# Four expert picks summed one query chunk earlier, and three groups of the state-space norm scaled by GpSimd

## The chip, the cores and the metric

The kernel runs on one core of a Trainium2 chip. The time is the device time of one execution in microseconds, as a median of several runs. The core's engines are TensorE (matrix products), VectorE, ScalarE and GpSimd (elementwise work; GpSimd also issues the gathers), and SyncE, which issues the other transfers. Each works through its own queue in order, and they wait for each other on semaphores. The profile calls them PE, DVE, ACT, POOL and SP.

## What is computed

Two decoder layers, all in float32, on 256 tokens of width 1024. The first one is a hybrid of gated linear attention and a state-space block, followed by a mixture of experts with product keys. The change touches the norm of the state-space block and the expert layer:

```python
y = y.reshape(Bsz, L, SSD_D_INNER) * jax.nn.silu(z)              # 2048 columns
y = rmsnorm(y.reshape(Bsz, L, SSD_GROUPS, SSD_D_INNER // SSD_GROUPS),
            ssd_norm_w.reshape(SSD_GROUPS, -1)).reshape(Bsz, L, SSD_D_INNER)   # 4 groups of 512
y_b = y.astype(hn.dtype) @ w_up_ssd
...
q = (hb @ w_q).reshape(n, PEER_HEADS, 2, PEER_HALF)              # 16 chunks of 128 query columns
s = jnp.einsum('nhid,hikd->nhik', q, sub_keys)
...                                                              # top 16 experts for each of 8 heads
u = jnp.take(u_tab, idx, axis=0)
act = jax.nn.gelu(jnp.einsum('nhkd,nd->nhk', u, hb))
out = jnp.einsum('nhk,nhkd->nd', w * act, jnp.take(v_tab, idx, axis=0))
```

The second part of the network (retention and stick-breaking attention) is not touched.

## The kernel before

All weights come as one stream of chunks of 128x1024 numbers. A chunk is loaded, split into a high half (ScalarE, line 1612) and a low half (VectorE, line 2072), and multiplied in three products (lines 1118 to 1120). Kind "T" chunks hold 128 columns (a chunk is 8 times 3 products of 256 columns), kind "N" chunks hold 512 columns of 256 rows. One generator, `order_of_work`, writes out the order of all steps once, and every engine's program walks the same list and issues its own part of each step. So a step's place in the list is its place in the queue of every engine that takes part in it. Side work is cut into strands, and a strand goes on at fixed places between the products of a chunk (`side_step`).

**The norm.** The gated features Y lie as two tiles of 128 tokens by 2048 columns. When a group's squares are summed (step `z`), VectorE computes the reciprocal root (step `y_root`, lines 1980 to 1992; groups 0 and 1 in one go, then 2, then 3) and multiplies the identity by it, once for each token tile: a diagonal (lines 1996 and 1997). TensorE then turns the features and scales them in one (step `yT`, sixteen of them, four in each group): two products of 128x128 float32 by the diagonal into a bank of PSUM, 4 to 7 in turn (lines 1383 and 1384). ScalarE and VectorE take high and low halves out of the bank (lines 1773 and 2287), and only then can the bank be used by the yT four places on. DY holds the diagonals of two groups, so the root of group 2 waits for the yT of group 0. The steps stand in this order: y_root 0 in chunk 83, y_root 2 and yT 0 and 1 in chunk 85, yT 2 and 3 in 86, yT 4 to 7 in 87, y_root 3 behind chunk 88, yT 8 and 9 behind 89, and so on. Chunks 73 to 88 are z, from 89 on comes the product with `w_up_ssd`.

**The expert layer.** A pick is one (token tile, head, rank): 256 picks, each for 128 tokens. GpSimd gathers 128 rows of 8 KB for it (line 2624), 1.05 MB, half of a row for the dot product and half for the sum. For each pick VectorE takes the dot (step `dot`, line 2371), ScalarE the gelu of four picks at a time (line 1823), VectorE multiplies by the softmax weights (step `weigh`, line 2376), ScalarE makes a diagonal of the weight (line 1831), and TensorE adds diagonal times rows to the output, two products of 512 columns (step `sum`, line 1434), each of which is two instructions. The gathers go into up to 17 slots. A slot is free for a new pick when the old pick's sum is done; slots that overlap the ring of split chunks are free when a certain query chunk has been multiplied. Before the change no sum stands in the list before the scores of the last two query chunks, step ("scores", 14, 2). The picks go into slots like this: picks 0 to 8 into slots 1, 2, 3, 7, 8, 6, 4, 5 and 0; 9 to 15 into slots 14, 10, 11, 12, 13, 15 and 16; pick 12 waits for chunk 14 of the query, 13, 14 and 15 for chunk 15; pick 16 goes into slot 9 (behind the scores of chunk 15), 17 to 20 into the slots of picks 0 to 3.

**The order around the last query chunks.** Chunk 14 (with the scores of 12 and 13 in its middle), dot 8, gelu of picks 4 to 7, gather 12; chunk 15, dot 9, weigh of 4 to 7, gathers 13 to 15; the scores of 14 and 15, dot 10, sums 0 to 7, gathers 16 to 24. The weights of picks 0 to 3 are made at dot 7, behind chunk 13. Scores are 8 products of 128x128 (line 1415); ScalarE copies each query chunk out of PSUM first (line 1801) and the scores afterwards (line 1810).

Of the kernel before, what the change touches and what calls it, by code (L numbers as in the profile page):

```python
# [11 lines left out]
ALU = mybir.AluOpType  # L12
# [165 lines left out]
def order_of_work():  # L178

    done = set()  # L180
# [416 lines left out]
    def peer_side():  # L597
# [28 lines left out]
        for m in range(256):  # L626
# [10 lines left out]
            if ("scores", 14, 2) not in done:  # L637
                for ms in waiting:
                    if ("weigh", *ms) not in done:
                        yield say("weigh", *ms)  # L640
            while waiting and ("scores", 14, 2) in done:
                yield from weighed()
# [280 lines left out]
def build(nc, stream, par, rows, con1, con2, xin, xt, meta, subk, peer_uv, out):  # L923
    ctx = ExitStack()
    with ctx:
# [19 lines left out]
        SM = sb("SM", [128, 512])  # L945
# [10 lines left out]
        def place(name, at, n):  # L956
            assert at + n <= ARENA, name
            return AR[:, at:at + n]
# [48 lines left out]
        ZS = place("ZS", 20944, 1024).rearrange("p (b c) -> p b c", b=2)  # L1007
        DY = place("DY", 0, 512).rearrange("p (b i c) -> p b i c", b=2, i=2)
        H = place("H", 25600, 2048).rearrange("p (i d) -> p i d", i=2)
# [102 lines left out]
        def tensor_program(pe, hi, lo, prod, side, act, dve, pool):  # L1112
# [38 lines left out]
            for step, *at in order_of_work():  # L1151
# [226 lines left out]
                elif step == "yT":  # L1378
                    f, = at
                    b, g, c = 4 + f % 4, f // 4, slice(128 * f, 128 * f + 128)  # L1380
                    on.wait_ge(*dve.of(("y_root", max(g, 1))))
                    bank(b)
                    pe.matmul(ps[b][:, 0:128], Y[:, 0, c], DY[:, g % 2, 0, :], start=True, stop=True)
                    pe.matmul(ps[b][:, 128:256], Y[:, 1, c], DY[:, g % 2, 1, :], start=True, stop=True).then_inc(*side.up(("yT", f)))
                    free[b] = dve.of(("yT", f))
# [585 lines left out]
        def vector_program(v, hi, lo, prod, side, act, dve, pool):  # L1971
# [58 lines left out]
            for step, *at in order_of_work():  # L2030
# [243 lines left out]
                elif step == "y_root":  # L2274
# [3 lines left out]
                    root(("y", g), SM[:, 16 + 2 * g:18 + 2 * groups[-1]], 512)  # L2278
                    if g >= 2:
                        on.wait_ge(*side.of(("yT", 4 * (g - 2) + 3)))  # L2280
                    for n in groups:
                        diagonals(("y_root", n), DY[:, n % 2, :, :], SM[:, 16 + 2 * n:18 + 2 * n])
                elif step == "yT":
# [317 lines left out]

        def pool_program(g, hi, lo, prod, side, act, dve, pool):
            on = Passed(g)
            uses = {}
            for step, *at in order_of_work():
                if step == "gather":
                    m, j, before = at
# [15 lines left out]
                    uses[j] = uses.get(j, 0) + 1  # L2623
                    g.indirect_dma_start(slots[j], None, peer_uv, bass.IndirectOffsetOnAxis(ap=IDX[:, i, c:c + 1], axis=0)).then_inc(s_uv[j], 16)  # L2624

# [230 lines left out]
```

## Time and profile before

| | |
|---|---|
| median of three runs | 1486.52 us (1486.42 to 1487.09) |
| profiled execution | 1488.33 us |
| its span, first to last instruction | 1486.5 us |
| TensorE busy | 1358.8 us, 91% |
| VectorE busy | 1064.0 us, 72% |
| ScalarE busy | 678.8 us, 46% |
| GpSimd busy | 298.0 us, 20%, all in issuing gathers |
| mean granted TensorE clock | 0.966 of full speed |

The profile is one execution. Its page gives the busy time of each engine, the span cut in 40 slices of 37 us, the chain of work that ended last, and groups of instructions by line. The trace behind it gives single instructions with start and duration, the idle time in front of each and the instruction that ended it. Times in it are us from the start of the span. The norm's steps lie between 306 and 342 us, the query chunks between 403 and 455, the picks between 417 and 1077.

### The profile page before, as it was taken

What the parts mean: (1) busy time and instruction counts of PE and PEld (TensorE: products, weight loads), DVE (VectorE), ACT (ScalarE), POOL (GpSimd) and SP (SyncE); (2) the same over time, 40 slices, a digit from 0 to 9 for tenths busy, and PEclk for the clock granted to TensorE, in tenths of its full rate; (3) what the DMA queues carried; (4) which work ended last, traced back from release to release, by engine and by line L of the source; (5) the groups of instructions that cost most, each with busy time, mean ns of one, the idle gap of its engine ahead of it and who ended that gap; (6) DMA issues with size and microseconds to landing.
All of it is one profiled execution on the core that took longest, in us unless ns stands there. A gap on an engine that the chain in (4) does not pass through costs nothing.

```text
span 1486.5 us, 18111 instructions
## 1 busy us (share of the span) xinstructions
PE 1358.8 (91%) x6713; PEld 980.8 (66%) x6713; DVE 1064.0 (72%) x2115; ACT 678.8 (46%) x1246; POOL 298.0 (20%) x260
## 2 busy tenths in 40 slices
PE   9999999999999887787878687788999999999998
PEld 9999989789895333333333233333499888998876
DVE  6977688766698777776777677665787665766664
ACT  7765976674553222222122222222364575645663
POOL 0000000000035554444435444443200000000000
PEclk9999999999999999998989989999999999999999
DMA  8444555445979999999999999999765555454542
GB/s 303 154 174 142 185 177 167 152 157 184 344 287 393 421 421 421 420 423 421 421 421 421 421 422 421 422 420 422 310 231 174 166 184 185 162 177 143 167 144 86
DMA packets 78487, 418.78 MB, mean 282 GB/s; under 512 B 8816, under 2 KB 9008, under 8 KB 45376
## 3 DMA queue, kind: packets, MB, share of 16 engines
q0 software_dynamic: 36864, 268.45, 43.6%
q1 hardware_dynamic: 41536, 149.17, 30.5%
q8 instruction: 54, 0.88, 0.2%
q14 instruction: 33, 0.27, 0.1%
HBM read 416.51 MB, written 1.08 MB: 281 GB/s over the span
## 4 chain that ended last, share of the span: by engine, by line
PE 58%; DMA 27%; DVE 9%; ACT 3%; issue 2%; POOL 1%; DVEq 0%; SPq 0%; POOLq 0%; ACTq 0%
DMA AR<-in_peer_uv,C 15%; PE ps L1118 14%; PE ps L1120 14%; PE ps L1119 14%; DMA SLAB<-in_peer_uv,C 12%; PE ps L1434 8%; DVE AR L2371 1%; DVE wlo L2072 1%; DVE SLAB L2371 1%; POOL SLAB L2624 1%; ACT whi L1612 1%; PE ps L1367 1%; POOL AR L2624 0%; ACT AR L1831 0%; DVE AR L2213 0%
## 5 line engine op out<-in xcount | busy, mean ns | idle before, releaser
L2072 DVE TENSOR_TENSOR wlo<-raw,whi 128x1024 fp32r<-128x1024 f32 x246 | 298.9, 1222 | 148.7 <-ACT whi L1612 148.0
L1434 PE MATMUL ps<-SLAB,AR 128*128 128x512 f32 x520 | 258.9, 650 | 59.5 <-ACT AR L1831 59.5
L1612 ACT ACTIVATE whi<-raw 128x1024 fp32r<-128x1024 f32 x246 | 258.9, 1057 | 118.8 <-PE ps L1120 103.7
L1434 PE MATMUL ps<-AR 128*128 128x512 f32 x504 | 248.3, 643 | 55.8 <-ACT AR L1831 55.6
L1118 PE MATMUL ps<-XH,whi 128*128 128x256 f32 (+1 forms) x896 | 261.6, 292 | 0.6 <-DVE XL L2312 0.6
L2624 POOL DMA_INDIRECT AR<-in_peer_uv,C x126 | 140.8, 1118 | 588.5 <-DVE C L2027 416.7
L1120 PE MATMUL ps<-XH,wlo 128*128 128x256 f32 (+1 forms) x896 | 254.2, 284 | 0.0
L1119 PE MATMUL ps<-XL,whi 128*128 128x256 f32 (+1 forms) x896 | 254.1, 284 | 0.0
L1434 PEld LDWEIGHTS ps<-SLAB,AR 128*128 128x128 f32 x520 | 105.3, 207 | 207.8 <-issue 125.3
L1434 PEld LDWEIGHTS ps<-AR 128*128 128x128 f32 x504 | 101.2, 205 | 197.2 <-issue 118.2
L2371 DVE CUSTOM_DVE_ANT_0 SLAB<-SLAB,AR 128x1024 f32<-128x1024 f32 x130 | 158.3, 1223 | 72.7 <-DMA SLAB<-in_peer_uv,C 72.7
L2371 DVE CUSTOM_DVE_ANT_0 AR<-AR 128x1024 f32<-128x1024 f32 x126 | 153.4, 1224 | 57.7 <-DMA AR<-in_peer_uv,C 57.7
L2624 POOL DMA_INDIRECT SLAB<-in_peer_uv,C x130 | 157.0, 1207 | 169.5 <-PE ps L1434 139.8
L1118 PEld LDWEIGHTS ps<-XH,whi 128*128 128x128 f32 x896 | 170.7, 191 | 2.9 <-issue 1.2
L1119 PEld LDWEIGHTS ps<-XL,whi 128*128 128x128 f32 x896 | 170.7, 191 | 1.5 <-issue 1.2
L1120 PEld LDWEIGHTS ps<-XH,wlo 128*128 128x128 f32 x896 | 170.6, 190 | 0.0
L1118 PE MATMUL ps<-whi,XH 128*128 128x512 f32 x416 | 170.4, 410 | 0.0
L1823 ACT ACTIVATE C<-C,SM 128x4 f32<-128x4 f32 (+2 forms) x75 | 22.2, 296 | 311.9 <-DVE C L2371 309.6
L1120 PE MATMUL ps<-whi,XL 128*128 128x512 f32 x416 | 162.6, 391 | 0.0
L1119 PE MATMUL ps<-wlo,XH 128*128 128x512 f32 x416 | 162.6, 391 | 0.0
L1831 ACT ACTIVATE AR<-C 128x128 f32<-128x128 f32 x248 | 82.1, 392 | 153.5 <-DVE C L2376 125.1
L1118 PEld LDWEIGHTS ps<-whi,XH 128*128 128x128 f32 x416 | 78.3, 188 | 17.1 <-issue 1.7
(407 smaller groups left out, 1720.7 us busy)
## 6 DMA issues: line engine op xcount, KB each, us to landing
raw<-in_stream SPq DMA_DIRECT2D x246, 512.0 KB, 3.8
AR<-in_stream SPq DMA_DIRECT2D x9, 512.0 KB, 8.1
AR<-scr SPq DMA_DIRECT2D x8, 512.0 KB, 4.8
SLAB<-in_peer_uv,C POOLq DMA_INDIRECT x130, 28.2
AR<-in_rows SPq DMA_DIRECT2D x4, 512.0 KB, 5.0
AR<-in_peer_uv,C POOLq DMA_INDIRECT x126, 28.2
AR<-in_con SPq DMA_DIRECT2D x1, 1280.0 KB, 6.7
AR<-in_xin SPq DMA_DIRECT2D x2, 512.0 KB, 9.5
```

What stands on the lines that cost most here:

```text
L1118: pe.matmul(o, sh, mh, start=first, stop=False)
L1119: pe.matmul(o, sh, ml, start=False, stop=False)
L1120: return pe.matmul(o, sl, mh, start=False, stop=last)
L1367: pe.matmul(ps[4][TOP, p], M[:, g % 2, i, r, TOP], XD[:, i, p], start=True, stop=True)
L1434: t = pe.matmul(ps[2 * i + half][:, :], d, rows_in[:, 512 * half:512 * half + 512], start=c == 0, stop=c == 127)
L1612: a.activation(in_two(whi[i % NS][:, :]), src, ACT.Copy).then_inc(*hi.up(i))
L1823: a.activation(CC[:, i, c], AV[:, i, c], ACT.Gelu_apprx_tanh, scale=SM[:, 24 + i:25 + i]).then_inc(*act.up(("gelu", at[0])))
L1831: a.activation(DG[:, m % 4, :], ident, ACT.Copy, scale=CC[:, i, c:c + 1]).then_inc(*act.up(("diagonal", m)))
L2072: v.tensor_tensor(in_two(wlo[i % NS][:, :]), src, in_two(whi[i % NS][:, :]).bitcast(F32), ALU.subtract).then_inc(*lo.up(i))
L2371: v.tensor_tensor_reduce(u, u, HN[:, i, :], 1.0, 0.0, ALU.mult, ALU.add, AV[:, i, c:c + 1]).then_inc(*dve.up(("dot", m)))
L2624: g.indirect_dma_start(slots[j], None, peer_uv, bass.IndirectOffsetOnAxis(ap=IDX[:, i, c:c + 1], axis=0)).then_inc(s_uv[j], 16)
```

## The change

Two things, independent of each other.

First, the condition on the sums: the group of picks 0 to 3 may be summed once the scores of chunks 12 and 13 stand in the list, all others as before. In the list this puts sums 0 to 3 behind dot 8, that is between query chunk 14 and chunk 15, in front of the gelu of picks 4 to 7. With four more free slots the gathers are dealt out otherwise: pick 12 into its slot as before, then picks 13 to 16 into the slots of picks 0 to 3 (waiting for their sums), 17 to 19 into the slots that wait for chunk 15, 20 into slot 9, 21 to 24 as before.

Second, for groups 0, 1 and 2 of the norm GpSimd multiplies Y by the roots in place, two instructions of 128x512 a group, and TensorE turns the scaled features with plain transposes. VectorE makes diagonals for group 3 only, and its root of group 2 doesn't wait for a yT any more. The yT of groups 0 to 2 wait for GpSimd's two instructions of their group. (The argument of `pool_program` is renamed from g to gp throughout.)

```diff
-            while waiting and ("scores", 14, 2) in done:
+            while waiting and ("scores", 14 if waiting[0][0] else 12, 2) in done:
                 yield from weighed()
...
-        DY = place("DY", 0, 512).rearrange("p (b i c) -> p b i c", b=2, i=2)
+        DY = place("DY", 0, 256).rearrange("p (i c) -> p i c", i=2)
...
                 elif step == "yT":
                     f, = at
                     b, g, c = 4 + f % 4, f // 4, slice(128 * f, 128 * f + 128)
-                    on.wait_ge(*dve.of(("y_root", max(g, 1))))
+                    on.wait_ge(*(dve.of("last_diagonals") if g == 3 else pool.of(("y_scaled", g))))
                     bank(b)
-                    pe.matmul(ps[b][:, 0:128], Y[:, 0, c], DY[:, g % 2, 0, :], start=True, stop=True)
-                    pe.matmul(ps[b][:, 128:256], Y[:, 1, c], DY[:, g % 2, 1, :], start=True, stop=True).then_inc(*side.up(("yT", f)))
+                    if g < 3:
+                        pe.transpose(ps[b][:, 0:128], Y[:, 0, c], ident)
+                        m = pe.transpose(ps[b][:, 128:256], Y[:, 1, c], ident)
+                    else:
+                        pe.matmul(ps[b][:, 0:128], Y[:, 0, c], DY[:, 0, :], start=True, stop=True)
+                        m = pe.matmul(ps[b][:, 128:256], Y[:, 1, c], DY[:, 1, :], start=True, stop=True)
+                    m.then_inc(*side.up(("yT", f)))
                     free[b] = dve.of(("yT", f))
...
                     root(("y", g), SM[:, 16 + 2 * g:18 + 2 * groups[-1]], 512)
-                    if g >= 2:
-                        on.wait_ge(*side.of(("yT", 4 * (g - 2) + 3)))
-                    for n in groups:
-                        diagonals(("y_root", n), DY[:, n % 2, :, :], SM[:, 16 + 2 * n:18 + 2 * n])
+                    if g == 3:
+                        diagonals("last_diagonals", DY, SM[:, 22:24])
...
+                if step == "y_root":
+                    g, = at
+                    if g == 3:
+                        continue
+                    on.wait_ge(*dve.of(("root", ("y", g))))
+                    for n in ((0, 1), (), (2,))[g]:
+                        for i in range(2):
+                            yg = Y[:, i, 512 * n:512 * n + 512]
+                            k = 16 + 2 * n + i
+                            gp.tensor_scalar(yg, yg, SM[:, k:k + 1], None, ALU.mult).then_inc(*pool.up(("y_scaled", n)))
```

## Rows read from the trace of the kernel before

**Rows 1.** Page, part 4: the chain that ended last, share of the span

```profile
PE 58%; DMA 27%; DVE 9%; ACT 3%; issue 2%; POOL 1%; DVEq 0%; SPq 0%; POOLq 0%; ACTq 0%
```

**Rows 2.** Page, part 2: GB/s of the DMA engines in 40 equal slices

```profile
GB/s 303 154 174 142 185 177 167 152 157 184 344 287 393 421 421 421 420 423 421 421 421 421 421 422 421 422 420 422 310 231 174 166 184 185 162 177 143 167 144 86
```

**Rows 3.** Timeline of TensorE, norm: start, us, line, out<-in, count [idle<-releaser]

```profile
314.88 0.38 PE L1383 MATMUL ps<-AR 128*128 128x128 f32 x2
315.09 0.39 PE L1384 MATMUL ps<-AR 128*128 128x128 f32 x2
...
322.46 0.49 PE L1383 MATMUL ps<-AR 128*128 128x128 f32 x2 [0.60 <-DVE XL L2287]
```

**Rows 4.** Timeline of TensorE, transposes of the h_turn steps, first and last of eight

```profile
401.85 0.27 PE L1397 MATMUL ps<-C,AR 128*128 128x128 f32 x1
...
402.61 0.27 PE L1398 MATMUL ps<-C,AR 128*128 128x128 f32 x1
```

**Rows 5.** Timeline of VectorE, around the roots of the norm

```profile
310.07 0.16 DVE L1992 SCALAR_TENSOR_TENSOR SM<-SM 128x4 f32<-128x4 f32 x1
...
312.57 0.69 DVE L2273 TENSOR_TENSOR AR<-AR 128x512 f32<-128x512 f32 x1 [0.17 <-ACT AR L1759]
...
319.61 0.29 DVE L1996 TENSOR_SCALAR AR<-C,SM 128x128 f32<-128x128 f32 x1
...
320.00 0.87 DVE L2287 SCALAR_TENSOR_TENSOR XL<-ps,PAR,XH 128x256 fp32r<-128x256 f32 x2
320.79 1.22 DVE L2072 TENSOR_TENSOR wlo<-raw,whi 128x1024 fp32r<-128x1024 f32 x1
```

**Rows 6.** Timeline of ScalarE, the high half of chunk 90

```profile
319.54 1.06 ACT L1612 ACTIVATE whi<-raw 128x1024 fp32r<-128x1024 f32 x1
```

**Rows 7.** Waits from 340 to 420, TensorE's: us in total, times, longest

```profile
PE ps L1118 <- DVE XL L2312: 0.6, 1, 0.6
```

**Rows 8.** Timeline of GpSimd: picks 0, 12 and 13, and one later gather

```profile
417.11 1.07 POOL L2624 DMA_INDIRECT AR<-in_peer_uv,C  x1 [416.66 <-DVE C L2027]
...
451.98 0.93 POOL L2624 DMA_INDIRECT SLAB<-in_peer_uv,C  x1 [2.46 <-PE ps L1120]
454.86 0.93 POOL L2624 DMA_INDIRECT SLAB<-in_peer_uv,C  x1 [1.94 <-PE ps L1120]
...
580.49 1.98 POOL L2624 DMA_INDIRECT SLAB<-in_peer_uv,C  x1 [0.31 <-issue]
```

**Rows 9.** Timeline of VectorE, a dot beside that later gather

```profile
580.43 1.22 DVE L2371 CUSTOM_DVE_ANT_0 SLAB<-SLAB,AR 128x1024 f32<-128x1024 f32 x1 [1.05 <-DMA SLAB<-in_peer_uv,C]
```

**Rows 10.** Timeline of TensorE from 440 to 1060: sums behind a wait (4 instructions each)

```profile
457.42 7.11 PE L1434 MATMUL ps<-AR 128*128 128x512 f32 x12 [1.22 <-ACT AR L1831]
...
534.09 3.78 PE L1434 MATMUL ps<-AR 128*128 128x512 f32 x4 [3.56 <-ACT AR L1831]
...
592.17 7.13 PE L1434 MATMUL ps<-SLAB,AR 128*128 128x512 f32 x16 [2.81 <-ACT AR L1831]
```

**Rows 11.** Timeline of VectorE, the weights of picks 0 to 3

```profile
454.26 0.16 DVE L2376 TENSOR_TENSOR C<-C 128x4 f32<-128x4 f32 x1
```

**Rows 12.** Timeline of ScalarE: copy of query chunk 14; diagonals of picks 0 to 3

```profile
451.75 0.37 ACT L1801 COPY AR<-ps 128x256 f32<-128x256 f32 x1 [0.59 <-PE ps L1120]
...
456.97 1.27 ACT L1831 ACTIVATE AR<-C 128x128 f32<-128x128 f32 x4
```

**Rows 13.** Line 2624, landing of the gathers issued at 417.11, 451.98, 454.86, 497.20

```profile
DMA to landing us min/median/max: 5.7/5.7/5.7
DMA to landing us min/median/max: 7.6/7.6/7.6
DMA to landing us min/median/max: 7.5/7.5/7.5
DMA to landing us min/median/max: 15.8/15.8/15.8
```

**Rows 14.** Windows: us, busy of each engine, granted clock, DMA share, GB/s

```profile
458.00:459.00 1.00, 1.00 (x3) 0.41 (x2) 1.00 (x4) 0.24 (x1) 0.69 (x2) 0.50 0.96 401
```

More of the change, by code:

```diff
@@ L2600, in vector_program, with pool_program @@
                             *dve.up(("out", tt, half)))
-        def pool_program(g, hi, lo, prod, side, act, dve, pool):
-            on = Passed(g)
+        def pool_program(gp, hi, lo, prod, side, act, dve, pool):
+            on = Passed(gp)
             uses = {}
             for step, *at in order_of_work():
-                if step == "gather":
+                if step == "y_root":
[8 more added lines that the diff above has]
+                            gp.tensor_scalar(yg, yg, SM[:, k:k + 1], None, ALU.mult).then_inc(*pool.up(("y_scaled", n)))
+                elif step == "gather":
                     m, j, before = at
@@ L2623, in pool_program @@
                     uses[j] = uses.get(j, 0) + 1
-                    g.indirect_dma_start(slots[j], None, peer_uv, bass.IndirectOffsetOnAxis(ap=IDX[:, i, c:c + 1], axis=0)).then_inc(s_uv[j], 16)
+                    gp.indirect_dma_start(slots[j], None, peer_uv, bass.IndirectOffsetOnAxis(ap=IDX[:, i, c:c + 1], axis=0)).then_inc(s_uv[j], 16)
         def sync_program(sp, hi, lo, prod, side, act, dve, pool):
```

## Prediction

> **What bounds the kernel now.** I read the page first. Of the chain that ended last 58% are TensorE and 27% DMA [rows 1]. The slices tell the two apart: in the first ten the DMA engines move 142 to 303 GB/s, in the fourteenth to the twenty-eighth 420 to 425 [rows 2]. The first stretch is TensorE's, the second, in which the 256 gathers run, belongs to DMA. The two halves of the change lie in one each, so each is priced by its own limit: the norm's by what it takes from TensorE's queue, the early sums by what they do to the stream of gathers.
>
> **Part 1, the norm of the state-space block.** *Removed from TensorE.* A yT step is now two products by a diagonal, and each is two instructions: L1383 x2 starts at 314.88 and L1384 x2 at 315.09, so one step is 4 starts of 0.11 us, 0.44 us [rows 3]. A transpose is one instruction: the eight of the h_turn steps start from 401.85 to 402.61, 0.11 us apart [rows 4]. A changed step is 2 x 0.11 = 0.22 us, so the twelve of groups 0 to 2 give 12 x 0.22 = 2.64 us back. That holds only where TensorE is not itself waiting, and it is at one place: yT 6 starts at 322.46 after 0.60 us for VectorE [rows 3], because it reuses the bank that VectorE's half of yT 2 must empty.
>
> What does the change do to that wait? VectorE loses two diagonals in front of its yT 0: L1996 at 319.61, its yT 0 at 320.00, so 0.39 us [rows 5]. But its next instruction, the low half of chunk 90 (L2072 at 320.79), waits for ScalarE's high half, 319.54 + 1.06 = 320.60 [rows 5, 6]. Of the 0.39 us only about 0.14 reach yT 2 (320.65 instead of 320.79). So at yT 6 TensorE is 0.14 us ahead of before and not 6 x 0.22 + 0.14: the time saved on yT 0 to 5 turns into a longer wait there. Behind it yT 6 and 7 give 0.44 and yT 8 to 11 give 0.88. Sum: 0.14 + 0.44 + 0.88 = **1.46 us**. From there to 402 TensorE has no other wait in the trace than one of 0.6 us on L1118, which sits behind its own results [rows 7], so what is gained at 333 is still there at the first gather. Here lies my choice: 1.46, with 2.64 as the far end if the wait at yT 6 went away too.
>
> *Added.* GpSimd gets six products of 128x512. It has done nothing until 417.11 [rows 8], so nothing is queued behind them before the gathers. Nothing in the trace shows GpSimd doing arithmetic. The nearest rows are VectorE's product of the same size, 0.69 us [rows 5], and GpSimd's own instructions, 0.93 us alone and 1.98 at the longest [rows 8, 9]. The roots of groups 0 and 1 end at 310.07 + 0.16 = 310.23 [rows 5], and yT 0 comes at 314.88 [rows 3]: two products have 4.65 us, 2.3 each, and the four of groups 0 and 1 have until 319.9, 2.4 each. Even 1.98 is covered, so I cost them at nothing; beyond 2.3 us each, every us costs two to four. The four diagonals of groups 0 and 1 leave VectorE's queue as well, but its next product (312.57) follows a result of ScalarE [rows 5], so that buys nothing. VectorE's root of group 2 no longer waits for yT 3 either; its row at 319.61 shows no idle time in front of it [rows 5]. Group 3 is as before.
>
> The Trainium skill, GPSIMD Engine Reference, section 3.1, gives 769 ns for a tight loop over 512 elements. By that figure the cover holds with room.
>
> **Part 2, four picks ahead of the last query chunk.** *Moved.* The sums of picks 0 to 3 (8 products by 512 columns, each two instructions; a group of four picks takes 7.13 us [rows 10]) go from behind the scores of chunk 15 to between chunks 14 and 15, and ScalarE's four diagonals with them. Picks 13 to 16 then go into the slots of picks 0 to 3 and wait for these sums; picks 17 to 19 wait for the end of chunk 15. The number of gathers in flight doesn't rise.
>
> Can TensorE start the sums there? The weights of picks 0 to 3 are made on VectorE behind the dot of pick 7: L2376 at 454.26, 0.16 us [rows 11], at the end of a queue in which VectorE's rows follow each other without idle time. Chunk 14 has ended when ScalarE copies it, 451.75 [rows 12]. So ScalarE's diagonals start at 454.45, and TensorE 0.45 us behind the first (456.97 to 457.42 [rows 10, 12]), at 454.9. **The new wait**: about 3.2 us on TensorE, in a stretch in which it now does chunk 15: the gathers that follow the ends of chunks 14 and 15 start at 451.98 and 454.86, 2.9 us apart [rows 8]. Behind it stand chunk 15 and its scores; behind ScalarE's wait for the weights stand the gelu of picks 4 to 7 and the copy of chunk 15. Then the sums, 454.9 to 461.9, chunk 15 to 464.8, the scores and the sums of picks 4 to 7 about 1.5 us later than now.
>
> What does that cost the gathers? Pick 13 is issued at 454.86 and its rows are there after 7.5 us, at 462.36; with nothing ahead of it a gather takes 5.7 us [rows 8, 13]. Changed, it waits for the first sum, 454.9 + 1.8 + 0.2 = 456.9, and lands at 462.6, some 0.3 later. Pick 14, at 458.7, could land at 464.4, before the queue is through with pick 13 (1.05 MB at 421 GB/s, 2.5 us): the stream is closed again. Pick 17, behind the end of chunk 15, is issued at 465.1 and could land at 470.8; the queue comes to it only at 462.6 + 4 x 2.5 = 472.6. So the shift of the stream is **+0.3 us**. Below, the best would be to fill what is still open in front of picks 13 and 14: pick 12, issued at 451.98, lands 7.6 us later at 459.6, pick 13 2.8 us behind it instead of 2.5, which I take twice: 0.6 us [rows 8, 13]. The holes before them belong to picks issued earlier and stay. Later steps of VectorE slip by 1 to 3 us, under a queue of gathers that take 15.8 us to land even behind the longest pause in issuing them (at 497.20 [rows 13]), so they cost nothing; without that cover they would cost in full.
>
> **Sum**: the profiled execution took 1488.33 us, its span 1486.5. 1488.33 - 1.46 + 0.3 = 1487.2. The median of the runs shown, 1486.52, is 1.8 lower, so the forecast is **1485.4**.
>
> **The rivals.**
> *The clock falls in the new wait.* Now the granted clock is 0.50 at 458 to 459, the lower level, after the gaps around the scores [rows 14], and the three picks from 457.42 take 7.11 us; after 3.56 us without work one pick at 534.09 takes 3.78 us; after 2.81 us at 592.17 four picks take 7.13, full speed [rows 10]. 3.2 us lies between. At half clock pick 0 takes 3.3 instead of 1.7 us, pick 13 is issued at 458.4, and the stream shifts by 0.3 + 1.5 = 1.8 us. Result 1485.4 + 1.5 = 1486.9.
>
> *GpSimd and VectorE get in each other's way.* A GpSimd instruction that starts beside a VectorE product with two inputs in SBUF (L2371 at 580.43) takes 1.98 us where one alone takes 0.93, and the VectorE one keeps its 1.22 [rows 8, 9]. Were it VectorE that waits, both of its z products (0.69 us, the first at 312.57 [rows 5]) could stand behind a scaling of about 1 us; both lie on the chain from ScalarE's z to the root of group 2, and so ahead of yT 6. That takes 1.5 us from part 1: 1486.9, with both rivals 1488.4. The Trainium skill, SBUF — State Buffer, "Who interferes with whom", states this rule: the shared port pair is an exclusive lock, a two-input VectorE instruction contends with a GpSimd one that reads SBUF, and the order of issue decides who waits. By it part 1 would come to about nothing; the trace has only the half in which GpSimd waits.
>
> *GpSimd is too slow* (the slower side): its place is yT 0 and yT 4, it decides from 2.3 us an instruction. At 4 us two are ready at 318.3 and four at 310.23 + 16 = 326.2, so yT 0 and again yT 4 wait, and yT 6, now at 322.46, comes at 326.6: +4.2, less 1.3 behind it, +2.9 in place of -1.46. With part 2 that gives 1489.7, above 1489.5. Against it: every elementwise 128x512 row above is 0.69 us, every GpSimd row under 2.
>
> *All is gained*: 2.64 and the 0.6 of the gathers, 1486.52 - 3.3 = 1483.2. It needs the wait at yT 6 gone, which the chain from ScalarE denies.
>
> *The change doesn't do what it says*: sums in front of the last chunk, but no gather earlier. By the times above this is the forecast itself.
>
> **Chances.** Forecast (-1.1) 30%; clock falls 24%; the two engines collide 16%, both 8%; GpSimd too slow 12%; all gained 10%. A measurement of this kernel can tell about 0.2%, 3.0 us, so faster is under 1483.5 and slower over 1489.5. Faster 0.10; within 0.78; slower 0.12. The range goes from 1483.0 to 1490.0.
>
> **What would show it.** L1383 as transposes, one instruction each, 0.22 us a step; six GpSimd rows before 330, each under 2 us, and VectorE's L2273 still 0.69 us; a wait of nearly 2 us at yT 6; the first gather at about 415.6; TensorE idle for 3.2 us before the first L1434, released by ScalarE, and the clock there; pick 13 issued 39.8 us behind the first gather (37.8 now). Wrong would make it: gathers issued closer together than now, a stall at yT 0, or a TensorE wait between 333 and 402.

## The result, and the profile after

The change made the kernel slower by a little: 1489.58 us, the median of 18 runs (1487.33 to 1491.13), against 1486.66 us before (18 runs, 1486.35 to 1488.70). The ratio is 1.0018, 95% interval [1.0011, 1.0024]. The forecast was 1485.4. The profiled execution after is the fastest of its 18: 1487.33 us, span 1485.4. So its trace shows the change at its best, and what the median adds to it has to be found elsewhere.

The chain that ended last doesn't tell the two kernels apart (page, part 4; TensorE 58% and DMA 27% in [rows 1]):

```profile
PE 59%; DMA 27%; DVE 9%; ACT 3%; issue 1%; POOL 0%; DVEq 0%; SPq 0%; POOLq 0%; ACTq 0%
```

**The norm.** Timeline of TensorE after, as [rows 3] of before (start us, us, line, operation; idle time before it and its releaser in brackets):

```profile
313.62 0.27 PE L1384 MATMUL ps<-C,AR 128*128 128x128 f32 x1
313.73 0.27 PE L1385 MATMUL ps<-C,AR 128*128 128x128 f32 x1
...
321.06 0.33 PE L1384 MATMUL ps<-C,AR 128*128 128x128 f32 x1 [1.52 <-DVE XL L2290]
```

A step is two instructions 0.11 us apart, as a transpose was in [rows 4], and the wait at yT 6 has grown from 0.60 to 1.52 us. GpSimd's six products, which no row of before shows, and VectorE beside them, as in [rows 5]:

```profile
309.08 6.53 POOL L2618 TENSOR_SCALAR AR<-AR,SM 128x512 f32<-128x512 f32 x4 [308.65 <-DVE SM L1997]
318.35 3.68 POOL L2618 TENSOR_SCALAR AR<-AR,SM 128x512 f32<-128x512 f32 x2 [2.73 <-DVE SM L1997]
```

```profile
309.41 1.43 DVE L2077 TENSOR_TENSOR wlo<-raw,whi 128x1024 fp32r<-128x1024 f32 x1 [0.43 <-ACT whi L1617]
311.32 0.69 DVE L2278 TENSOR_TENSOR AR<-AR 128x512 f32<-128x512 f32 x1 [0.48 <-ACT AR L1764]
313.49 0.69 DVE L2278 TENSOR_TENSOR AR<-AR 128x512 f32<-128x512 f32 x1 [1.48 <-ACT AR L1764]
```

The six GpSimd products take 1.57, 1.63, 1.55, 1.82, 1.56 and 2.14 us, all under the 2.3 of the cover. VectorE's two z products keep their 0.69 us; only one split of weights, L2077, takes 1.43 instead of 1.22. Who waits for whom is seen in the single products (narrow windows of the same timelines):

```profile
313.80 1.82 POOL L2618 TENSOR_SCALAR AR<-AR,SM 128x512 f32<-128x512 f32 x1
319.89 2.14 POOL L2618 TENSOR_SCALAR AR<-AR,SM 128x512 f32<-128x512 f32 x1
```

```profile
319.38 1.23 DVE L2077 TENSOR_TENSOR wlo<-raw,whi 128x1024 fp32r<-128x1024 f32 x1 [0.34 <-ACT whi L1617]
```

Each of these two starts while VectorE is inside a product with two inputs, with 0.38 us of it left (the z product from 313.49 to 314.18) and 0.72 us (the split from 319.38 to 320.61). They are 0.26 and 0.58 us longer than the 1.56 of those that start outside one: it is GpSimd that waits. The other way round, VectorE's split at 319.38 and both z products start while GpSimd is inside a product, and they lose nothing.

**The early sums.** TensorE's first sum after [rows 10], and GpSimd's picks 0, 12 and 13 to 16 [rows 8]:

```profile
452.26 5.42 PE L1439 MATMUL ps<-AR 128*128 128x512 f32 x12 [3.21 <-ACT AR L1836]
```

```profile
414.47 1.15 POOL L2637 DMA_INDIRECT AR<-in_peer_uv,C  x1 [92.43 <-DVE C L2032]
...
449.33 0.94 POOL L2637 DMA_INDIRECT SLAB<-in_peer_uv,C  x1 [2.43 <-PE ps L1120]
454.52 1.05 POOL L2637 DMA_INDIRECT AR<-in_peer_uv,C  x1 [4.26 <-PE ps L1439]
456.24 1.70 POOL L2637 DMA_INDIRECT AR<-in_peer_uv,C  x1 [0.66 <-PE ps L1439]
458.25 1.99 POOL L2637 DMA_INDIRECT AR<-in_peer_uv,C  x1 [0.30 <-issue]
460.54 0.94 POOL L2637 DMA_INDIRECT SLAB<-in_peer_uv,C  x1 [0.30 <-issue]
```

The wait of 3.21 us is there, the clock stayed up in this execution (5.42 us for three picks; [rows 10] has 7.11 at half clock), and pick 13 is issued 454.52 - 414.47 = 40.05 us behind the first gather (39.8 forecast, 37.75 before). What the forecast did not have is in the windows. First the kernel before, then after, in pairs of microseconds that lie equally far (37 to 43 us) behind the first gather of each (us, busy time of TensorE, its loads, VectorE, ScalarE and GpSimd, granted clock, share of the DMA engines, GB/s):

```profile
454.11:456.11 2.00, 1.54 (x12) 1.24 (x11) 1.80 (x11) 0.62 (x2) 0.95 (x2) 1.00 0.90 320
456.11:458.11 2.00, 0.78 (x3) 0.33 (x3) 2.00 (x4) 1.87 (x6) 1.70 (x2) 0.93 0.97 393
458.11:460.11 2.00, 2.00 (x4) 0.97 (x3) 2.00 (x6) 0.13 (x1) 1.09 (x2) 0.50 1.01 424
```

```profile
451.47:453.47 2.00, 1.21 (x3) 0.68 (x4) 1.80 (x11) 1.46 (x5) 0.00 (x0) 1.00 1.00 397
453.47:455.47 2.00, 2.00 (x6) 0.85 (x5) 2.00 (x4) 0.00 (x0) 0.95 (x1) 1.00 0.60 250
455.47:457.47 2.00, 2.00 (x6) 0.85 (x5) 2.00 (x6) 0.00 (x0) 1.34 (x2) 1.00 0.57 131
```

Before, the DMA engines are hardly ever without work; after, they run dry. In these three windows (320 + 393 + 424) - (397 + 250 + 131) = 359 GB/s times 2 us are missing, 0.72 MB, which is 1.7 us at the stream's 421 GB/s [rows 2]. Later hardly anything more is lost. In the 60 us from the first gather on, the gathers' queue (q0 in the DMA view of that stretch) moved 21.53 MB before and 20.78 MB after; in 600 us, 248.22 and 247.49 MB. That is 0.75 and 0.73 MB less, so the whole loss arises in these windows.

**Where the whole time lies.** Three marks split every trace of this study: the first transposition of the norm (yT 0), the first gather, and the last gather. Worked out from the timelines of TensorE and GpSimd (us; the profiled execution of each kernel; labels are those of the experiments below):

| kernel | first gather behind yT 0 | last gather behind first | span's end behind last gather |
|---|---|---|---|
| before | 102.23 | 637.21 | 432.18 |
| after | 100.85 | 638.75 | 432.18 |
| after, again (e5) | 100.83 | 640.81 | 432.25 |
| norm alone (e1) | 100.84 | 636.91 | 432.14 |
| sums alone (e2) | 102.22 | 641.25 | 432.21 |
| sums alone, wait filled (e6) | 102.19 | 639.10 | 432.20 |
| after, wait filled (e3) | 102.38 | 638.80 | 432.17 |
| after, weights early (e4) | 100.83 | 636.45 | 432.23 |
| sums, weights early (e7) | 102.22 | 637.06 | 432.12 |
| one chunk more (e8) | 102.41 | 637.54 | 432.24 |
| norm alone, filled (e9) | 101.82 | 636.74 | 432.13 |
| after, early, filled (e10) | 101.84 | 637.11 | 432.11 |
| products in the wait (e11) | 99.44 | 636.62 | 432.13 |
| GpSimd on one column (e12) | 100.86 | 636.73 | 432.20 |

The last column doesn't move: nothing of the change reaches the part behind the gathers. The first belongs to the norm, the second to the sums. Two cautions on the second. The kernels e4, e10 and e11 have the same steps behind the norm, and their values go from 636.45 to 637.11: one profiled execution can't tell differences under some 0.7 us. And the execution of before had a fall of the clock of its own, behind the wait of 1.22 us in front of its first sum (7.11 us for three picks [rows 10]). In e1, e9 and e12 the sums stand in the same order behind the same wait, and the clock stayed up; here e1's first sum:

```profile
454.75 5.42 PE L1439 MATMUL ps<-AR 128*128 128x512 f32 x12 [1.22 <-ACT AR L1836]
```

Their streams take 636.73 to 636.91 us instead of 637.21. What is left in the whole time, the time of yT 0 itself, is 313.3 to 314.9 us and varies between executions of programs that are equal up to there.

### The profile page after: what moved, and what is told of

Its sections match the earlier page's. It is cut to its first block, busy times and chain, and to the rows that moved or that the text cites. A ratio compares the mean times of both kernels' runs of the same rounds, so it can differ in the third digit from the quotient of the medians.

```text
span 1485.4 us, 18064 instructions
## 1 busy us (share of the span) xinstructions
PE 1349.5 (91%) x6689; PEld 974.9 (66%) x6689; DVE 1062.6 (72%) x2109; ACT 678.0 (46%) x1246; POOL 302.4 (20%) x266
## 4 chain that ended last, share of the span: by engine, by line
PE 59%; DMA 27%; DVE 9%; ACT 3%; issue 1%; POOL 0%; DVEq 0%; SPq 0%; POOLq 0%; ACTq 0%
DMA AR<-in_peer_uv,C 15%; PE ps L1118 14%; PE ps L1119 14%; PE ps L1120 14%; DMA SLAB<-in_peer_uv,C 12%; PE ps L1439 9%; DVE AR L2374 2%; DVE wlo L2077 1%; DVE SLAB L2374 1%; ACT whi L1617 1%; PE ps L1367 1%; ACT AR L1836 0%; DVE AR L2218 0%; PE ps L1351 0%; DVE AR L2008 0%
## 5 line engine op out<-in xcount | busy, mean ns | idle before, releaser
L2077 DVE TENSOR_TENSOR wlo<-raw,whi 128x1024 fp32r<-128x1024 f32 x246 | 299.0, 1222 | 147.6 <-ACT whi L1617 147.2
L1439 PE MATMUL ps<-AR 128*128 128x512 f32 x508 | 243.4, 625 | 48.2 <-ACT AR L1836 48.0
L2637 POOL DMA_INDIRECT AR<-in_peer_uv,C x127 | 145.1, 1143 | 254.9 <-PE ps L1439 136.8
L2637 POOL DMA_INDIRECT SLAB<-in_peer_uv,C x129 | 146.9, 1139 | 186.2 <-PE ps L1439 160.0
```

Of the source, the lines that this page charges most:

```text
L1439: t = pe.matmul(ps[2 * i + half][:, :], d, rows_in[:, 512 * half:512 * half + 512], start=c == 0, stop=c == 127)
L2077: v.tensor_tensor(in_two(wlo[i % NS][:, :]), src, in_two(whi[i % NS][:, :]).bitcast(F32), ALU.subtract).then_inc(*lo.up(i))
L2637: gp.indirect_dma_start(slots[j], None, peer_uv, bass.IndirectOffsetOnAxis(ap=IDX[:, i, c:c + 1], axis=0)).then_inc(s_uv[j], 16)
```

## The experiments

The theory, once the two traces were compared: the norm part gives its 1.4 us; the early sums cost twice, once because the stream of gathers runs dry while picks 13 to 16 wait for sums that wait for their diagonals, and once more because in most executions the granted clock falls behind that wait (the trace of after happens to be one in which it doesn't). The rivals: only one of the two is real; the norm part costs as well; or the new order of the slots costs something at the end of the stream.

**e1 and e2: one half each.** e1 keeps the norm part and has the old condition for the sums; e2 is the kernel before with this line alone:

```diff
-            while waiting and ("scores", 14, 2) in done:
+            while waiting and ("scores", 14 if waiting[0][0] else 12, 2) in done:
```

> The kernel before with the norm's part alone. Both profiles have run-to-run noise at their start, but from the roots of the norm to the first gather the changed kernel gained 1.4 us. If the norm's part is as forecast (each transpose pair 0.22 us, GpSimd's products hidden) the ratio is 0.999, 1.4 us faster than before, and its times spread as little as those of before. If GpSimd's products cost something that this one trace does not show, it is 0 to 2 us slower.

> The kernel before with the early sums alone. The traces show the stream of gathers 1.6 us later behind the new wait without a fall of the clock. Theory of the dry stream: +1.6 us and no more. Theory of the clock: in most executions TensorE falls to the lower clock in the wait of 3.2 us, the first sums come 1.5 us later still, so +3 to +4.5 us with a spread of some us between executions. Theory of the slots: the picks rotate through the slots in another order, the last ring slots are freed at sum 238 instead of 234, and the loss lies at the end, around 1030 to 1080, not at 455.

Norm alone: 1486.34 us against 1487.02 on that chip, ratio 0.9995 [0.9986, 1.0004]; the interval holds 1, so the norm's gain is shown by the marks of the traces and not by the times. Sums alone: 1490.53 us, ratio 1.0023 [1.0014, 1.0032]. The two differences, -0.7 and +3.5, make +2.8, the whole change's +2.9. So the loss is the sums'. It does not come from the slots at the end: e2's gathers' queue is 1.58 MB behind that of before 60 us after the first gather, and 1.52 MB 600 us after it. In e2's trace the clock fell. First sum and windows:

```profile
453.71 7.12 PE L1434 MATMUL ps<-AR 128*128 128x512 f32 x12 [3.18 <-ACT AR L1831]
```

```profile
454.00:455.00 1.00, 1.00 (x3) 0.36 (x3) 0.92 (x5) 0.72 (x3) 0.00 (x0) 0.75 0.93 377
455.00:456.00 1.00, 1.00 (x3) 0.48 (x2) 1.00 (x2) 0.00 (x0) 0.00 (x0) 0.50 0.96 393
456.00:457.00 1.00, 1.00 (x2) 0.36 (x2) 1.00 (x3) 0.00 (x0) 0.00 (x0) 0.50 0.30 123
457.00:458.00 1.00, 1.00 (x2) 0.33 (x1) 1.00 (x4) 0.00 (x0) 0.98 (x1) 0.54 0.06 25
```

A wait of 3.18 us, as in after's 3.21, but behind it the lower level, 1.2 GHz (0.50), for some 3 us; the products of three picks take 7.12 us, the gathers come later still, and the stream ends 641.25 us behind its first gather, 4.0 later than before.

**e3 and e6: work in the wait.** Fourteen products of the unit matrix in front of the first sum, into the bank that it overwrites; e3 in the changed kernel, e6 in the kernel with the sums alone:

```diff
                     h, k = divmod(c, 16)
+                    if m == 0:
+                        bank(2)
+                        for _ in range(14):
+                            pe.matmul(ps[2][:, 0:128], ident, ident, start=True, stop=True)
```

> The changed kernel with 14 products of the identity by itself (0.22 us each) on TensorE in the new wait, into a bank that nobody reads then; the sums start no earlier. Theory of the clock: the clock stays up, the spread goes and the median falls by 1.5 to 3 us against the changed kernel, to +0.2 us against before. Theories of the dry stream or of the slots: no change by the filling, it stays 2.7 us slower than before.

> The kernel before with the early sums alone (the old norm), and in front of sum 0 fourteen products of the 128x128 unit matrix with itself into the bank that sum 0 is about to overwrite: the same values leave the kernel, and TensorE has work in the wait. The sums alone gave 1490.5 us with the clock at 0.50 behind the wait and the last gather 641.25 us behind the first. Theory (clock and dry stream are two separate losses, about 2.2 and 1.7 us): clock 1.00, last gather 638.8 to 639.2 us behind the first, time 1488.3 to 1488.8. Rival one (the fall of the clock costs nothing, since the stream is bound by transfers): 641.2 us and 1490.5. Rival two (the clock is all of the loss): 637.2 us and 1487.0.

e6: 1488.88 us against 1487.16, ratio 1.0011 [1.0001, 1.0020], the stream 639.10 us long, the clock 1.00. So of the sums' 3.5 us the clock is 3.5 - 1.7 = 1.8 us in the medians, and 641.25 - 639.10 = 2.15 us in the traces; the dry stream is the other 1.7 (639.10 - 637.21 = 1.9 in the traces). Each median's interval reaches 1.4 us to either side, so this split rests on the traces. Both rivals, that the clock is all of the loss or none of it, are out: they asked for streams of 637.2 and 641.2 us. e3: 1487.52 us, 2.1 us below the changed kernel's median, ratio 1.0004 [0.9995, 1.0013].

e3's trace showed something that no theory had. Its first gather comes 102.38 us behind yT 0, as if the norm part gave nothing. The windows there:

```profile
321.00:322.00 1.00, 0.62 (x5) 0.44 (x5) 1.00 (x3) 1.00 (x4) 1.00 (x1) 0.97 0.39 33
322.00:323.00 1.00, 1.00 (x5) 0.81 (x3) 1.00 (x2) 0.86 (x3) 0.35 (x1) 0.50 0.52 172
```

Behind the wait of 1.5 us at yT 6, which the change lengthened from 0.60, the clock falls too, and takes 1.5 us, the whole gain of the norm part. It did so in two of the seven profiled executions that have this wait (e3 and e8). e3's eleven times fall in two groups that lie as far apart: eight from 1487.25 to 1487.79, three from 1488.81 to 1489.11, and the profiled one is of the second. That the other two of the three are such cases is an inference.

**e5: the changed kernel again**, to see whether one kernel is found at both levels.

> The changed kernel itself, once more with a profile. Its own profiled execution was the fastest of its 18 and kept the granted clock at 1.00 through the wait in front of the early sums, which does not go with a median 2.2 us above it. Theory (in most executions the clock falls to 0.50 in that wait): the twelve products of sum 0 take about 7.1 us instead of 5.42, pick 13 goes out 41 to 42 us behind the first gather instead of 40.05, and the last gather is issued 640.5 to 641.5 us behind the first instead of 638.75; the span is about 1487.5. Rival (the clock stays up, and the spread of the executions is from elsewhere): 5.42 us, 40.1 us and 638.8 us again, whatever the span. One execution may fall on either side; taken with the spread of the times it says whether the two levels are found in one kernel.

1489.05 us, span 1487.2. TensorE's three picks took 7.11 us behind a wait of 3.20. GpSimd's picks 12 to 14 and the window in which the stream was empty:

```profile
449.00 0.93 POOL L2637 DMA_INDIRECT SLAB<-in_peer_uv,C  x1 [2.45 <-PE ps L1120]
455.21 1.17 POOL L2637 DMA_INDIRECT AR<-in_peer_uv,C  x1 [5.28 <-PE ps L1439]
457.60 1.14 POOL L2637 DMA_INDIRECT AR<-in_peer_uv,C  x1 [1.22 <-PE ps L1439]
```

```profile
455.14:457.14 2.00, 2.00 (x4) 0.72 (x3) 2.00 (x6) 0.00 (x0) 1.17 (x1) 0.74 0.17 49
```

Same program, same wait: pick 13 goes out 41.07 us behind the first gather instead of 40.05, and the stream takes 640.81 us instead of 638.75. So the clock is worth 2.1 us here. By time, 16 of the 18 runs of after lie at 1488.8 or above, like this one; the profiled one of after is one of the two others. The share, most executions, is read from the times; traces show one at either level.

**e4 and e7: take the wait away.** The weights of picks 0 to 3 are made right behind their Gelu, one query chunk earlier on VectorE; e4 in the changed kernel, e7 with the old norm:

```diff
                 yield say("gelu", *ms)
                 waiting.append(ms)
+                if ms[0] == 0:
+                    yield say("weigh", *ms)
```

> The changed kernel with the weights of picks 0 to 3 made on VectorE straight behind dot 6, in front of the top-k of the next head and of dot 7, some 3 us earlier. The wait on TensorE between chunks 14 and 15 should be under 0.5 us, pick 13 issued some 36.7 us behind the first gather (40.1 in the changed kernel, 37.8 before). If the wait is the cause (dry stream and clock both): 1.5 to 2.5 us faster than before. If the slots are the cause: still slower than before.

> The kernel before with the early sums alone (the old norm), and with the weights of picks 0 to 3 calculated right behind their Gelu, one query chunk earlier; nothing is left out. Theory (what cost was the wait for the diagonals, which delays picks 13 to 16 until the queues are empty and lets the clock fall): both losses are gone and the sums in front of the last chunk even win: pick 13 goes out 37.6 us behind the first gather, the last gather 636.3 to 636.6 us, time 1486.0 to 1486.5, 0.6 to 0.9 us under the kernel before. Rival (the earlier place of the sums costs in itself, by the queries and scores of the last chunk that come 3.8 us later, and the run with both was carried by the norm part): 1487.3 to 1488, last gather 637.5 us or more behind the first.

e4: 1485.42 us against 1487.02, ratio 0.9989 [0.9980, 0.9998]. Its first sum, picks 12 to 14, and two windows of the same place:

```profile
450.27 5.42 PE L1441 MATMUL ps<-AR 128*128 128x512 f32 x12 [0.76 <-ACT AR L1838]
```

```profile
449.78 0.94 POOL L2639 DMA_INDIRECT SLAB<-in_peer_uv,C  x1 [2.43 <-PE ps L1122]
452.53 0.94 POOL L2639 DMA_INDIRECT AR<-in_peer_uv,C  x1 [1.81 <-PE ps L1441]
454.24 1.79 POOL L2639 DMA_INDIRECT AR<-in_peer_uv,C  x1 [0.78 <-PE ps L1441]
```

```profile
454.00:455.00 1.00, 1.00 (x3) 0.38 (x2) 1.00 (x2) 0.00 (x0) 0.76 (x1) 1.00 0.99 418
455.00:456.00 1.00, 1.00 (x4) 0.42 (x3) 1.00 (x3) 0.00 (x0) 1.00 (x1) 1.00 1.09 451
```

The wait is 0.76 us instead of 3.21 (under 0.5 was expected), pick 13 goes out 37.61 us behind the first gather (before: 37.75; 36.7 was expected), the stream is never dry and takes 636.45 us, 0.8 less than before. e7 has the same wait and pick 13 at 37.62, and a stream of 637.06 us, but its time, 1487.48 us against 1487.16, is no gain: ratio 1.0002 [0.9992, 1.0012]. The forecasts, 1486.0 to 1486.5 us and a stream of 636.3 to 636.6, were too good; the time lies in the rival's range, the stream doesn't (637.5 or more). Three pairs of kernels differ in the early sums with early weights alone: their medians differ by +0.3 us (e7 against before), -0.9 (e4 against e1) and, from the experiments below, +0.3 (e10 against e9). So without their wait the early sums cost nothing measurable, and gain nothing measurable either; whether a few tenths of e4's gain are theirs is not shown.

**e8: earlier still.** Gelu and weights behind dot 5, the four sums behind dot 7, so that picks 12 to 15 take the four slots:

```diff
-            while waiting and ("scores", 14 if waiting[0][0] else 12, 2) in done:
+            while waiting and ("scores", 14 if waiting[0][0] else 10, 2) in done and m >= 7:
...
-            behind = 1 if ("scores", 10, 2) in done else 3
+            behind = 1 if ("scores", 10, 2) in done else 3 if ("gelu", 0, 1, 2, 3) in done else 2
```

> The changed kernel with Gelu and weights of picks 0 to 3 behind dot 5, and their sums behind dot 7, in front of the chunk before the last; nothing is left out. The queues have holes from 439 to 448 us in every kernel so far, since gathers wait there for a free slot; here picks 12 to 15 take the four slots of picks 0 to 3 from about 449 us. Theory (the stream runs from its last hole on at the rate of the transfers, so that an earlier refill shifts it all): pick 12 goes out 34 to 35 us behind the first gather, the last gather 634.5 to 636 us, time 1483.9 to 1485.2. Rival (the diagonals aren't ready in front of that chunk: table load, four row scales and the weights on VectorE stand behind the top-8 of the first picks): TensorE waits 1 to 3 us, the clock may fall, and the time is 1486 to 1488.

1487.82 us against 1487.16, ratio 1.0003 [0.9994, 1.0013]: the rival. The diagonals are late again, TensorE waits 2.49 us for them, pick 12 goes out 35.57 us behind the first gather and not 34 to 35, and the stream takes 637.54 us. The profiled execution has the fall of the clock at yT 6 besides (102.41 us).

**e9, e10 and e12: the norm part's own costs.** e9 (norm alone) and e10 (changed kernel with early weights) fill the wait at yT 6:

```diff
                     b, g, c = 4 + f % 4, f // 4, slice(128 * f, 128 * f + 128)
                     on.wait_ge(*(dve.of("last_diagonals") if g == 3 else pool.of(("y_scaled", g))))
+                    if f == 6:
+                        bank(2)
+                        for _ in range(13):
+                            pe.matmul(ps[2][:, 0:128], ident, ident, start=True, stop=True)
```

> The norm part alone, and in front of the seventh transposition (the one that waits 1.52 us for the bank since the transpositions are short) thirteen products of the 128x128 unit matrix with itself into another bank; the same values leave the kernel. Two of ten profiled executions (the filled wait and the one-chunk-more kernel) had the clock at 0.50 for about 3.5 us behind this wait and the first gather 102.4 us behind the first transposition instead of 100.84. Theory (in a part of its executions the norm part loses its gain to the clock): filled, no execution has it; first gather 100.85 us behind the first transposition, median 0.4 to 0.8 us under that of the norm alone against the same kernel before (ratio 0.9987 to 0.9992), and the times lie within 1 us of each other but for single ones. Rival (the spread of 2 us is from the start of the execution): median and spread of the norm alone, 1485.3 to 1487.4.

> The changed kernel with the weights of picks 0 to 3 one chunk earlier, and the same thirteen products in front of the seventh transposition. Theory: both waits in which the clock can fall are closed (0.76 us in front of sum 0 was too short to do it in either profile); first gather 100.85 us behind the first transposition, last gather 636.4 behind the first, time 1485.2 to 1485.5 against 1485.4, and fewer executions at 1486.5 or more. Rival (the other executions' 1.2 us are from elsewhere): the same share of executions, 3 of 11, above 1486.4.

The filling was made too long. TensorE's timeline of e9:

```profile
319.36 3.07 PE L1385 MATMUL ps<-C 128*128 128x128 f32 x26
322.26 0.27 PE L1388 MATMUL ps<-C,AR 128*128 128x128 f32 x1
```

Thirteen products are 26 instructions (each product is two, unlike a transpose), 2.9 us in place of 1.5, and so yT 6 comes late and the first gather 101.82 us behind yT 0: 1.0 us of each time below is the filling's. e9: 1486.08 us, 0.26 below e1 where 0.4 to 0.8 was expected, against 1487.01, ratio 0.9993 [0.9984, 1.0002], and all eleven runs lie within 1.15 us of each other (1485.83 to 1486.98) where e1's lie within 2.2 (1485.25 to 1487.43). The narrower spread is what the theory asks for; less the filling's 1.0 the median would be 1485.1, an estimate. e10: 1486.38 us (1485.2 to 1485.5 expected; less the filling's 1.0 it would be 1485.4), ratio 0.9998 [0.9989, 1.0007], its stream 637.11 us where 636.4 was expected; again 3 of 11 runs stand apart, at 1487.0 to 1487.6, as 3 of 11 of e4 do at 1486.5 to 1486.7. There the rival holds: with the wait filled the clock at yT 6 doesn't explain those executions, and their cause stays open.

e12 lets GpSimd's products run over one column instead of 512:

```diff
-                            yg = Y[:, i, 512 * n:512 * n + 512]
+                            yg = Y[:, i, 512 * n:512 * n + 1]
```

> The norm part alone, with GpSimd's six products over one column instead of 512. What it leaves out: 511 of 512 elements of each row are not scaled. Theory (GpSimd's 10.2 us lie beside work of the others and cost only 0.2 us on one split of VectorE, which TensorE doesn't wait for): first gather 100.8 us behind the first transposition as with the whole products, and that split takes 1.22 us instead of 1.43. Rival (they delay VectorE's part of the transpositions and so keep some of the gain): the first gather comes 0.2 us or more earlier, at most 100.6.

GpSimd and VectorE at that place:

```profile
309.47 2.01 POOL L2618 TENSOR_SCALAR AR<-AR,SM 128x1 f32<-128x1 f32 x4 [309.04 <-DVE SM L1997]
310.00 1.23 POOL L2618 TENSOR_SCALAR AR<-AR,SM 128x1 f32<-128x1 f32 x1
```

```profile
309.80 1.28 DVE L2077 TENSOR_TENSOR wlo<-raw,whi 128x1024 fp32r<-128x1024 f32 x1 [0.43 <-ACT whi L1617]
```

The second row is the third of the four instructions by itself. It starts inside VectorE's split (309.80 to 311.08), ends just behind it and takes 1.23 us, where the other five take 0.27 to 0.29: GpSimd waited for VectorE here too. The split of weights takes 1.28 us instead of 1.43, and the first gather comes 100.86 us behind yT 0, as with the whole products (100.84), behind the same wait of 1.52 us at yT 6. So GpSimd's 10.2 us cost TensorE nothing.

**e11: useful work in the wait.** The wait at yT 6 filled with work that has to be done anyway, the two steps of the z group that stood behind yT 7, on top of e4:

```diff
             if j == 1:
                 yield PAUSE
+                if g == 1:
+                    yield PAUSE
```

> The changed kernel with the weights of picks 0 to 3 one chunk earlier, and the six products of the next z group (128x512, 1.4 us of TensorE) issued in front of the seventh transposition instead of behind the eighth; nothing is left out. Theory (the transpositions' gain is cut by a wait for the bank, whose reader on VectorE stands behind 2.3 us of splits of weights): the wait falls from 1.52 us to under 0.3, the first gather comes 99.5 to 99.9 us behind the first transposition instead of 100.84, and the time is 1484.0 to 1484.6. Rival (VectorE or the first products of the out projection are the late ones behind it, and wait for the transposed groups): the 1.3 us turn up as a wait in front of the out projection at about 328 us, and the time is 1485.2 to 1485.6.

TensorE's timeline of e11:

```profile
320.41 0.40 PE L1124 MATMUL ps<-whi,XL 128*128 128x512 f32 x1
320.94 0.33 PE L1388 MATMUL ps<-C,AR 128*128 128x128 f32 x1
```

The last of the six products starts at 320.41, yT 6 at 320.94: 0.53 us behind it, where these products follow each other at 0.23, so about 0.3 us of the 1.52 is left. The rival's wait in front of the out projection is not there; TensorE's only other wait up to 400 is the 0.6 us of before [rows 7]. The first gather comes 99.44 us behind yT 0, 2.8 us less than before. The time is 1484.15 us (1483.55 to 1485.08) against 1487.01, ratio 0.9981 [0.9972, 0.9990]. The place of the first gather and the time are those of the theory (a little beyond it: 99.5 to 99.9 expected). It is the fastest version here, 2.9 us under the kernel before where the changed kernel is 2.9 over it.

## Why the prediction was wrong

*The norm part: right.* 1.46 us forecast for the first gather, 102.23 - 100.85 = 1.38 measured. The step that cut 2.64 down to it, the saved time of yT 0 to 5 turning into a wait at yT 6, stands in the trace: 1.52 us, a little less than the "nearly 2" of the forecast. No wait on TensorE was added from 333 to 402 [rows 7].

*GpSimd's cover: right.* 1.55 to 2.14 us; the longest is over the 1.98 taken as the upper bound, but below the 2.3 from which it would cost. The rival of a GpSimd that is too slow (12%) is out. The Trainium skill, GPSIMD Engine Reference, section 3.1, gives 769 ns for a tight loop over 512 elements; these products take 1.56 us where nothing is in their way, twice as long, and the measurement decides.

*The two engines in each other's way: present, but not as the rival feared, and harmless.* The rival needed VectorE's z products to wait behind GpSimd; they kept 0.69 us. It is GpSimd that waits when it starts inside a VectorE product with two inputs: 0.26 and 0.58 us in the two cases above, 0.95 in e12. Of the five splits and z products that start while GpSimd is inside a product, four lose nothing and one loses 0.2 us. With e12 the cost at the first gather is nil. The Trainium skill, SBUF — State Buffer, "Who interferes with whom", calls the shared port pair an exclusive lock and lets the order of issue decide who waits; the traces agree where VectorE comes first, and show at most 0.2 us of it where GpSimd does.

*The early sums' times: right.* Wait 3.21 us (3.2 forecast), pick 13 at 40.05 us (39.8), pick 13's rows 45.65 us behind the first gather against 45.25 before, 0.4 later (0.3 forecast).

*The early sums' price, +0.3 us: this is the step that failed.* It took the landing of pick 13 for the shift of the whole stream and counted on "the stream is closed again" with pick 14. But a gather that lands 5.6 us after its issue instead of 7.5 is faster because the queue is empty, and while the engines are idle nothing is moved of the picks behind it. Before, the gathers' queue had moved 15.29 MB when pick 13 landed, 0.6 MB more than picks 0 to 13 hold; after, 14.95 MB, 0.3 MB more, and 0.4 us later. The right count is the bytes that are not moved in the hole, 1.7 us of them in the windows above. The rest of the step held: picks 14 and 15 took 1.70 and 1.99 us to issue beside VectorE's dots and landed 6.6 and 7.8 us after their start, yet opened no further hole. The stream's shift at full clock was 638.75 - 637.21 = 1.54 us, in e6 1.89; against e1 and e12, whose clock stayed up at the sums, 638.75 - 636.91 = 1.84 and 638.75 - 636.73 = 2.02.

*The clock: a rival at 24% where it is the usual case.* Its mechanism was right and its size near: 1.5 us forecast for the half-speed sums, 2.06 measured between the two traces of the changed kernel. But its whole price carried the same +0.3, so it too came out too low: a stream 1.8 us longer, where 3.60 was measured (e5). The odds were taken from two rows, a pick at half clock behind 3.56 us and picks at full clock behind 2.81 [rows 10]. With 3.2 us it fell in two of three profiled executions, and by the times in most.

*The same mechanism in part 1 was not in the forecast at all*: the longer wait at yT 6, on which the 1.46 rests, is itself one in which the clock may fall. Two of seven executions lost 1.5 us there.

*The sum.* The forecast was 1486.52 - 1.46 + 0.3 = 1485.4. With the sizes of the traces, -1.38 at the norm and, with the clock fallen, +3.60 in the stream, it is 1486.66 - 1.38 + 3.60 = 1488.9; with the fall at yT 6 besides, 1490.4. The median is 1489.58, between the two. This last assignment is arithmetic, not seen: no trace caught both falls in one execution.

## What to carry to other kernels

When a transfer stream is the limit, price a later issue by the bytes that its hole leaves unmoved, not by when the first late transfer lands. Before a consumer is moved forward, move forward what it waits for: the sums cost 3.5 us with their weights where they were and nothing measurable with the weights one chunk earlier. And time that is taken out of TensorE in front of a fixed wait is not a saving but a longer wait, with the clock at risk; move later work into it, as e11 does, and it becomes one.

## What the hardware showed

- Behind TensorE waits of 3.2 us the granted clock fell to 0.50 in two of three profiled executions, behind 1.52 us in two of seven, behind 1.22 us in one of four (before; not e1, e9, e12). Behind one wait of 2.49 us and four of 0.76 us it stayed at 1.00. The same program does both (after and e5), so one profile can show the kernel without its main loss.
- A GpSimd product in place by a column of factors took 1.56 us for 128x512 and 0.28 us for 128x1. Started inside a VectorE product with two inputs it took longer, by 0.12 to 0.14 us less than what was left of that product (0.26 and 0.58 us in after, 0.95 in e12). VectorE, starting beside such a GpSimd product, lost nothing in four of five cases.
- The issue of a gather waits for VectorE's dot in the same way. In the trace of before 108 gathers start inside a dot with more than 0.13 us of it left: 94 of them end 0.81 us behind the dot's end (0.79 to 0.83), so that the 0.93 us become up to 1.99; the other 14 start within a few ns of the dot's own start and take 0.94 us.
